# A hybrid encoder layer with 16 experts on one core: the last expert's rows stay on chip and reach the output by one-hot products

## The reference

```python
def grouped_moe(x, w_router, router_bias, wg, wu, wd):
    ...
    combine = jnp.einsum('tk,tke->te', w, jax.nn.one_hot(idx, N_EXPERTS, dtype=jnp.float32)).astype(x.dtype)
    y = jnp.zeros_like(xt)
    for e in range(N_EXPERTS):
        h = jax.nn.silu(xt @ wg[e]) * (xt @ wu[e])
        y = y + combine[:, e:e + 1] * (h @ wd[e])
    return y.reshape(shp)
...
        return layer_norm(ALPHA * x + y, ln2_g[l], ln2_b[l])
```

## Time and profile before

| what | us |
|---|---|
| median of 3 runs | 1161.46 |
| lowest, highest | 1157.88, 1167.65 |
| the profiled execution, its own time | 1164.74 |
| its span, first to last instruction | 1163.1 |
| PE, DVE, ACT, POOL busy in it | 1043.3, 894.6, 718.1, 188.7 |

### The profile page before, as it was taken

The page is one execution under the profiler, slowest core; times in us unless marked ns, Lnnn a source line. Parts: engine busy times, 40 slices in busy tenths (PEclk is TensorE's granted clock), DMA queues, the critical chain, the costliest instruction groups (busy, mean ns, idle before and its releaser), DMA issues.

```text
span 1163.1 us, 16849 instructions
## 1 busy us (share of the span) xinstructions
PE 1043.3 (90%) x5403; PEld 875.7 (75%) x5403; DVE 894.6 (77%) x1148; ACT 718.1 (62%) x887; POOL 188.7 (16%) x162
## 2 busy tenths in 40 slices
PE   5999999969989999999389999998799999999950
PEld 4988888857878888887278878887677888888840
DVE  2696674579978999887757858646897888888956
ACT  2424765356868888877524266734576888787852
POOL 3000000016421101110020000000372311221100
PEclk9999889979989999999799999899899999999985
DMA  9423120339999999997734222020799999999934
GB/s 316 160 80 110 40 78 19 110 103 318 366 344 379 387 385 384 385 375 303 222 103 145 81 83 92 27 101 27 248 303 381 376 381 392 379 379 378 374 120 163
DMA packets 117061, 273.27 MB, mean 235 GB/s; under 512 B 10304, under 2 KB 13344, under 8 KB 116992
## 3 DMA queue, kind: packets, MB, share of 16 engines
q1 hardware_dynamic: 101232, 236.80, 56.6%
q0 software_dynamic: 14464, 33.01, 8.1%
q10 hardware_dynamic: 1296, 2.62, 0.6%
HBM read 262.02 MB, written 25.22 MB: 247 GB/s over the span
## 4 chain that ended last, share of the span: by engine, by line
PE 57%; DMA 17%; DVE 10%; issue 6%; ACT 4%; DVEq 3%; POOL 3%; SPq 0%; ACTq 0%; POOLq 0%
DMA raw_far<-in_w_gate 9%; PE bankA L2093 9%; PE bankA L1801 8%; PE bankB L2093 7%; PE bankB L1801 7%; PE bankC L2116 5%; PE bankD L2116 5%; PE bankC L1801 3%; POOL slot_rows L727 3%; PE bankD L1801 3%; PE bankG L1881 3%; DVE w_lo L453 2%; PE bankE L1789 2%; PE bankF L1789 2%; ACT w_hi L447 2%
## 5 line engine op out<-in xcount | busy, mean ns | idle before, releaser
L453 DVE TENSOR_TENSOR w_lo<-raw,w_hi 128x2048 fp32r<-128x2048 f32 (+1 forms) x152 | 340.7, 2261 | 57.1 <-ACT w_hi L447 54.1
L447 ACT ACTIVATE w_hi<-raw 128x2048 fp32r<-128x2048 f32 (+1 forms) x152 | 287.1, 1893 | 120.9 <-PE bankC L1801 40.9
L453 DVE TENSOR_TENSOR w_lo<-raw_far,w_hi 128x2048 fp32r<-128x2048 f32 x64 | 146.4, 2288 | 14.5 <-ACT w_hi L447 14.5
L447 ACT ACTIVATE w_hi<-raw_far 128x2048 fp32r<-128x2048 f32 x64 | 122.8, 1919 | 46.8 <-PE bankB L2093 22.6
L2093 PE MATMUL bankA<-w_hi,xe_hi 128*128 128x512 f32 x256 | 100.7, 394 | 3.4 <-DVE xe_lo L468 3.2
L2093 PE MATMUL bankB<-w_hi,xe_hi 128*128 128x512 f32 x256 | 102.8, 402 | 0.6 <-DVE w_lo L453 0.6
L2093 PE MATMUL bankB<-w_hi,xe_lo 128*128 128x512 f32 x256 | 100.1, 391 | 0.0
L2093 PE MATMUL bankA<-w_hi,xe_lo 128*128 128x512 f32 x256 | 99.9, 390 | 0.0
L2093 PE MATMUL bankB<-w_lo,xe_hi 128*128 128x512 f32 x256 | 99.8, 390 | 0.0
L2093 PE MATMUL bankA<-w_lo,xe_hi 128*128 128x512 f32 x256 | 99.8, 390 | 0.0
L707 POOL DMA_INDIRECT y_rows<-expert_out,idx x32 | 47.9, 1495 | 189.0 <-ACT expert_out L1005 181.3
(11 more groups left out here) (430 smaller groups left out, 2459.5 us busy)
## 6 DMA issues: line engine op xcount, KB each, us to landing
raw<-in_w_up SPq DMA_DIRECT2D x64, 1024.0 KB, 11.3
raw_far<-in_w_gate SPq DMA_DIRECT2D x60, 1024.0 KB, 12.3
raw<-in_w_down SPq DMA_DIRECT2D x60, 1024.0 KB, 12.3
raw<-in_w_in SPq DMA_DIRECT2D x12, 1024.0 KB, 8.8
raw<-in_w_o SPq DMA_DIRECT2D x8, 1024.0 KB, 5.5
x_rows<-x POOLq DMA_DIRECT2D x10, 512.0 KB, 3.0
raw<-in_w_gate SPq DMA_DIRECT2D x4, 1024.0 KB, 8.2
raw_far<-in_w_down SPq DMA_DIRECT2D x4, 1024.0 KB, 12.3
```

The costliest lines, as they stand in the source:

```text
L447: act.activation(w_hi[:, s % RB, :, 0:n], raw_unit(s)[:, :, 0:n], ACT.Copy).then_inc(hi_done, 1)
L453: dve.tensor_tensor(w_lo[:, s % RB, :, 0:n], raw_unit(s)[:, :, 0:n], w_hi[:, s % RB, :, 0:n].bitcast(F32), ALU.subtract).then_inc(lo_done, 1)
```

## The change

Expert 15's output is never scattered. It is always a row's second expert, so:

- ACT and DVE split banks C and D of expert 15 into `xe_hi` and `xe_lo` (`last_hi`, `last_lo`), which stay on chip.
- POOL, in its program behind expert 11, makes five one-hot matrices `place_of[t]` [128 slots, 128 rows] from the slot list (`places`), from a copy of an iota that it loads.
- PE multiplies `place_of[t]` by `xe_hi` and `xe_lo` into two banks per tile (`last_rows`: G and H for even tiles, C and D for odd), and adds `y_second[t]` to them by a product with the identity (`second_rows`) for tiles 0 to 2 in layer 0 and for all in layer 1; DVE adds `y_second` itself for tiles 3 and 4 of layer 0. DVE adds the banks to `x` (`add_last`).
- Rows that have no scattered second output must read zero, so POOL writes zeros to all second rows of `y_rows` in each layer, by nine DMAs of 64 rows of 4 KB, right behind the store of `gv`.
- SP issues the loads of both outputs of a tile together, once expert 14's scatter has landed; the last waits for the turned hidden rows of 15.
- Down of expert 14 comes ahead of up of 15, on PE and in the order of the units. ACT and DVE follow.
- Of the next layer's first four units, two are split before `last_hi` and `last_lo` and two later; before, all came ahead of the sums but for the last `w_lo`. The first additions move into DVE's loop, two tiles ahead. PE runs 10 spare products behind down of 15. On ACT `root(0)` moves behind two copies.

The core of the diff:

```diff
+            def gate_or_up(l, s, w, e, i=0):
+                for k in range(2):
+                    load_expert(l, s + k, w[l, e, k * HALF:(k + 1) * HALF, :].rearrange("(t p) n -> p t n", t=4), i)
+
...
-                gate_up(l, SO_LAST, NE - 1)
-                down(l, SO_LAST + 4, NE - 2)
+                gate_or_up(l, SO_LAST, w_gate, NE - 1)
+                down(l, SO_LAST + 2, NE - 2)
+                gate_or_up(l, SO_LAST + 4, w_up, NE - 1)
                 down(l, SO_LAST + 6, NE - 1)
 
                 def block_units(e, b, ran):
...
-                    load_outputs(j)
+                sp.wait_ge(out_free[1], (NE // 2) * (l + 1))
+                sp.sem_inc(held_sp, 1)
+                sp.wait_ge(out_free[0], (NE // 2) * (l + 1) + 1)
+                sp.sem_inc(held_sp, 1)
+                for t in range(NT):
+                    load_output(t, 0)
+                    if t == NT - 1:
+                        wait_filled(sp, "ht", l, 0, NE - 1)
+                        sp.sem_inc(held_sp, 1)
+                    load_output(t, 1)
 
             for t in range(NT):
...
+                hold(zero_out, 16)
+                for a in range(0, SEQ + DEC, DEC):
+                    pool.dma_start(y2_dram[2 * a:2 * a + 2 * DEC, :].rearrange("(p j) n -> p j n", j=2)[:, 1, :],
+                                   zero_dram[0].partition_broadcast(DEC)).then_inc(second_zero, 16)
...
                 for e in range(NE):
                     if e + 4 < NE:
                         gather_next(e + 4)
-                    send(e)
+                    if e < NE - 1:
+                        send(e)
+                    else:
+                        pool.sem_inc(out_free[1], 1)
+                    if e == NE - 5:
+                        places()
 
                 def block_rows(e, b, ran):
 
...
                         round_end(i, c, s)
-                round_of(0, NE - 1, SO_LAST)
-                expert_rows_out(0, NE - 2)
-                hidden_hi(0, NE - 1)
+                last = NE - 1
+                split_hi(act, l, SO_LAST + 4, after="half")
+                hidden_hi(0, last - 1)
+                split_hi(act, l, SO_LAST + 5, after="gate", c=last)
+                gate(0, last)
+                split_hi(act, l, SO_LAST + 6, after="half")
+                expert_rows_out(0, last - 1)
+                split_hi(act, l, SO_LAST + 7, after="down1", c=last - 1)
+                hidden_hi(0, last)
                 def block_act(e, b, ran):
                     def hi(dst, src, after):
...
 
+                def last_hi():
+                    for h in range(2):
+                        hi_out(act, f"down{h}", l, t_cols(xe_hi, h, 1), hi_y, 0, NE - 1)
+
...
-                    expert_rows_out(0, NE - 1)
-                    with act.If(l < DEPTH - 1):
-                        for s in range(2, RB):
-                            next_split(s)
-                    act.sem_inc(held_act, 1)
-
-                overflow(act, l, past, block_act, held_act, after_blocks, lambda: expert_rows_out(0, NE - 1), no_blocks)
...
                         split_lo(dve, l, s + 9, i)
-                round_of(0, NE - 1, SO_LAST)
+                split_lo(dve, l, SO_LAST + 4)
+                hidden_lo(0, NE - 2)
+                split_lo(dve, l, SO_LAST + 5)
+                split_lo(dve, l, SO_LAST + 6)
+                split_lo(dve, l, SO_LAST + 7)
+                hidden_out(0, NE - 1)
                 hidden_lo(0, NE - 1)
 
...
+
+                def next_splits(units):
+                    with dve.If(l < DEPTH - 1):
+                        for s in units:
+                            split_lo(dve, l + 1, s)
+
+                def after_blocks(ran):
...
+                    last_lo()
+
+                overflow(dve, l, past, block_dve, held_dve, after_blocks, last_lo, no_blocks)
 
 
...
                     dve.sem_inc(held_dve, 1)
+                    add_output(t, 1, y_second[:, t, :])
+
+                def add_last(t):
                     n = P if t < 4 else DEC
-                    add_output(t, 1, y_second[:, t, :], accum_out=mv[0:n, t, 0:1])
-                    dve.drain()
-                    dve.tensor_scalar(mv[:, t, 0:1], mv[:, t, 0:1], -1.0 / D, None, ALU.mult).then_inc(mean_done, 1)
+                    dve.drain()
+                    for h in range(2):
+                        name = ("last", t, h)
+                        wait_filled(dve, name, l)
+                        part = x[0:n, t, h * HALF:(h + 1) * HALF]
+                        read(dve.scalar_tensor_tensor(out=part, in0=bank_of(name)[0:n, :], scalar=w12[0:n, t, 1:2], in1=part,
+                                                      op0=ALU.mult, op1=ALU.add, accum_out=sq[0:n, t, h:h + 1]), name)
+                    dve.drain()
+                    dve.tensor_scalar(mv[:, t, 0:1], sq[:, t, 0:1], sq[:, t, 1:2], -1.0 / D, ALU.add, ALU.mult).then_inc(mean_done, 1)
 
...
-                    for s in range(RB - 1):
-                        split_lo(dve, l + 1, s)
-
                 def tail(more):
                     dve.wait_ge(table2_in, 32 * l + 32)
                     dve.sem_inc(held_dve, 1)
-                    dve.drain()
-                    for t in range(NT):
+                    dve.memset(sq[DEC:P, NT - 1, :], 0.0)
+                    dve.drain()
+
+                    def add_before(t):
                         add_first(t)
-                    dve.memset(mv[DEC:P, NT - 1, 0:1], 0.0)
-                    dve.drain()
...
 
-                    add_second(0)
+                    add_before(0)
+                    add_before(1)
+                    add_last(0)
                     for t in range(NT):
+                        if t + 2 < NT:
+                            add_before(t + 2)
                         if t + 1 < NT:
-                            add_second(t + 1)
-
+                            add_last(t + 1)
                         dve.wait_ge(square_done, NT * l + t + 1)
                         dve.sem_inc(held_dve, 1)
                         centre_2(t)
...
                     if 2 <= t + 1 < NT:
                         turn_rows(l, t + 1)
-                    if t == 0 and between:
+                    if t == 0 and between is not None:
                         warm_products(5)
                     wait_read(pe, ("xt", t, 1), l)
                     projection(l, 0, t)
+                    if between is not None and t + SECOND_ON_PE < NT:
+                        between(t + SECOND_ON_PE, True)
                     if t == 0:
                         turn_rows(l, 1)
...
                         down(s + 4, i, c - 1)
-                round_of(0, NE - 1, SO_LAST)
-                down(SO_LAST + 4, 0, NE - 2)
+                wide("gate", SO_LAST, 0, NE - 1)
+                hidden_turn(0, NE - 2)
+                down(SO_LAST + 2, 0, NE - 2)
+                wide("up", SO_LAST + 4, 0, NE - 1)
                 hidden_turn(0, NE - 1)
...
+                overflow(pe, l, past, block_pe, held_pe, blocks_read)
+
+                def last_rows(t, stop=False):
+
+                    n = P if t < 4 else DEC
+                    for h in range(2):
+                        name = ("last", t, h)
+                        wait_free(pe, name, l)
+                        pe.sem_inc(held_pe, 1)
+                        wait_read(pe, f"down{h}", l, 0, NE - 1)
+                        for k, y in enumerate((xe_hi, xe_lo)):
+                            ins = pe.matmul(bank_of(name)[0:n, :], place_of[t][:, 0:n], t_cols(y, h, 1),
+                                            start=(k == 0), stop=(stop and k == 1))
+                        if stop:
+                            done(ins, name)
+
+                def second_rows(t):
+
+                    n = P if t < 4 else DEC
+                    pe.wait_ge(y_second_in[t], 16 * l + 16)
+                    pe.sem_inc(held_pe, 1)
+                    for h in range(2):
+                        name = ("last", t, h)
+                        done(pe.matmul(bank_of(name)[0:n, :], ident[0:n, 0:n], y_second[0:n, t, h * HALF:(h + 1) * HALF],
+                                       start=False, stop=True), name)
+
+                wait_free(pe, ("last", 0, 0), l)
+                for _ in range(10):
+                    pe.matmul(bank_of(("last", 0, 0))[:, :], h_hi[:, 0, 0:P], h_hi[:, 0:2, :], start=True, stop=True)
+                pe.wait_ge(places_done, l + 1)
+                pe.sem_inc(held_pe, 1)
+                last_rows(0)
+                last_rows(1)
+                second_rows(0)
+                second_rows(1)
 
                 with pe.If(l < DEPTH - 1):
+                    for t in range(2, SECOND_ON_PE):
+                        last_rows(t)
+                        second_rows(t)
                     wait_unit(pe, l + 1, 0)
                     wait_free(pe, ("proj", 0, 0), l + 1)
                     pe.sem_inc(held_pe, 1)
-                    pe.wait_ge(y_second_in[0], 16 * l + 16)
```

(8 more changed lines are left out.)

86 lines of the change are left out of this document (62 added, 24 removed).

## The result

The changed kernel takes 1203.72 us (median of 4 runs, 1201.61 to 1204.19), the kernel before 1163.51 beside it (4 runs). The ratio is 1.035, its 95% interval 1.0319 to 1.0382. Forecast were 1175 us and a range from 1156 to 1185: the sign is right, the size is a third of what came, and the time lies 19 us above the range. The profiled run of the change has a span of 1202.6 us, 39.5 more than that of before.

What follows compares the result with a forecast made beforehand. PE was taken as the bound, with 27 us of scatter and `y_second` waits at the layer ends, DVE next. Terms 8.5 - 0.5 + 5.4 = +13.4 us gave 1178.1 profiled, 1175 us forecast, range 1156 to 1185.

Steps and rivals of the forecast that it cites:

- the zeros, +5.4: At the first scores: zero writes delay the mask by 3.8 us in layer 1, 1.6 in layer 0; bounds 0 and 11.
- Rival (c): At the first scores: zeros cost the upper bound of 11 us in place of 5.4, giving 1180.5 us; chance 0.15.
- The loop of waits, +8.5: Layer 0's tail and next head: DVE and PE wait for each other around the projections, 8.5 us more; bounds +5 and +13.
- The order, +3.3 a layer: Last experts: down of 14 ahead of up of 15 makes down of 15 end 3.3 us later in each layer.
- The early means: Layer ends: without the scatter, tile 0's mean comes 5.6 us earlier in layer 0 and 5.0 in layer 1.
- layer 1's tail: After down of 15: additions in DVE's loop give most back; layer 1 in all -0.5 us, bounds -4 and +3.
- `root(0)`: "nothing": On ACT: moving `root(0)` behind two copies costs nothing.
- `places`, the wait for the zeros: On POOL: `places` ahead of the scatter of 12, and the wait for long-landed zeros, cost nothing; 3 us without that cover.

Runs made afterwards that it cites:

- Experiment 11: Changed kernel with zeros later, placing products before projection 0, old expert order, last layer's branch first, 22 spare products, `root(0)` back: 1156.06 us, ratio 0.9971.
- experiment 2: Kernel before, plus only the nine DMAs of zeros per layer at the change's place, read by nothing: 1177.28 us, ratio 1.0118.
- experiment 1: Changed kernel with the nine DMAs of zeros moved behind the load of `ln1_shift`, some 10 us later: 1187.08 us, ratio 1.0186.
- experiment 12: Kernel before, plus only down of 14 ahead of up of 15 on PE, ACT, DVE and in the unit order: 1161.31 us, ratio 0.9977.
- experiment 6: Changed kernel with PE's branch of the last layer written ahead of the branch with the next head: 1202.61 us, ratio 1.0323.

## Why the prediction was wrong

Of the change's 40 us, by what undoing each part gave: zeros 16.6, order 9.7, loop of waits 9.7, `root(0)` 4.9; sum 40.9. Experiment 11 took them all out, and ratio 1.035 became 0.997. Each of the four is uncertain by some 6 us, and by ratios they are 19, 12, 10 and 5, so that the sum comes within 1 us of 40 is luck.

In the profiled runs the sum had +13.4 us and +39.5 came, 26.1 more. By the table they are: 9.4 up to gate of 15 of layer 0 (11.0 for the 1.6 of the zeros), 4.7 from there to the turning of tile 4 (13.2 for 8.5), 2.3 from there to the second group of projections, where PE's idle time grew by 3.3, 4.2 at layer 1's scores (8.0 for 3.8), 3.5 from them to gate of 15, and 2.0 from there to the end (1.5 for -0.5).

**The step that failed most: the zeros, +5.4.** The mechanism was right (the mask lands late, and the first scores wait 12 us in layer 1), the term was mis-sized. Between the ends 0 and 6.7 us for the delay I took 3.8, for a third taker in turns; the mask landed 6.8 us later (15.3 for 8.5), which is the upper end. The zeros start 3 us ahead of the mask and POOL goes on issuing them for 1.3 us behind it; the delay is what it would be if nearly all of them were served first. And of layer 0's share I counted 2.2 us as hidden by the wait of the next scores; in experiment 2 the first scores come 7.0 us later and the next ones 6.9. The wait of the next scores, 1.85 us in the earlier trace rows, is still 1.74 there: PE makes them only when the first ones have been read, so that wait moves along and covers nothing. The term should have been 14 (6.8 in each layer); experiments 2 and 1 give 14.4 and 16.6. Rival (c) had this mechanism, with 11 as its upper bound, which the hidden share kept too low.

**The loop of waits, +8.5, was right in kind and short.** Both gaps came as forecast (6.65 and 6.38 us for 6.3 each), and projection 0 started 0.9 us earlier behind gate of 15 for 1.4 forecast. What came on top is the clock: I gave 1.2 us for a slower projection 2; the 4.8 us idle ahead of projection 0 cost 2.9 there, and the turns of tiles 3 and 4 and the projections in between another 2. From gate of 15 the turn of tile 4 comes 13.2 us later. That wait could have been read from the sum's own terms, in which 6.8 us lie between tile 0's being ready and its low rows; but I put a slow clock only where the kernel before had one.

**The order, +3.3 a layer.** Layer 0: 3.2. Layer 1: 4.8, the difference being down of 14 at the granted clock of 0.80. With the new order gate to down of 15 takes 22.4 or 24.0 us, whichever the layer: 24.0 in three of seven traces in layer 0 and in six of seven in layer 1. The sum had 0.3 for slow products. What I hadn't asked is what the order is good for: experiment 12 shows that beside the scatter of 15 it gives back up to 5.5 us at the first mean for the 3.2, and the change takes that scatter away. Both halves of the change attack one wait; with the first, the second has nothing left but its price.

**The early means were right**: counted from gate of 15, 5.8 us in layer 0 for 5.6 and 4.0 in layer 1 for 5.0; counted from down of 15, 9.0 and 8.9 us. In layer 1's tail I forecast that the additions in the loop would give most of it back: from down of 15 to the end 36.4 us are left of 39.8, 3.3 less, for a forecast of 3.8 less (0.5 and the 3.3 of the order).

**`root(0)`: "nothing" was wrong**, by 4.9 us in the total and 3.9 by the traces. I named no work that hides it, because it looked like two copies changing places. The price isn't in ACT's time, it is in PE's clock three steps on.

**`places`, the wait for the zeros**: next to nothing, as forecast. The rounds of the experts in which `places` runs take 18.1 us in both layers; the same rounds took 18.1 and 18.3 before.

Open: the idle time at the second group of projections (4.91 us for 1.59) is 2.9 to 5.4 us in all variants with PE's new program and 1.0 to 2.1 in those of the kernel before; experiment 6 didn't settle it.

## What to carry to other kernels

Bulk writes that nobody waits for yet still stand ahead of a small load that somebody waits for: price them at the whole time of their bytes unless something shows otherwise, and put them behind it. When an engine waits longer in a place, count the products that follow at the lower clock, also where two small operations on another engine only changed places. Before two measures are joined, ask whether they buy the same wait; the order of the last experts could pay only while expert 15 was scattered. And when a wait is removed, count the work that had run in it: here the first additions moved into the loop behind, and the loop grew by more than half of what the earlier start gave (5.5 us for 8.3 in layer 1).

## What the runs showed of the hardware

- The 24 products of tile 1 with `w_o` took 8.8 to 13.3 us in the eight traces with the moved root, behind a wait of some 2.5 us, and 7.2 to 7.6 us in the six without it, where PE didn't wait ahead of them; one of those twelve, experiment 2 in layer 0, took 8.9. I hadn't expected that 2.5 us of waiting could cost up to 6 us of slower products.
- The clock can fall without any difference in the program. In the traces of the kernel before and of experiment 12, which differ only in the last experts, PE is busy for 8.69 us of the 10 from 120 to 130 in both. From 130 on the granted clock is 0.50 in the one and 1.00 in the other, and the first product with `w_o` comes 4.4 us apart (139.51 and 135.12). Over the 14 traces that stretch, from layer 0's first scores, takes 31.5 to 37.6 us; a difference of a few us between two traces shows nothing by itself.
- The Trainium skill (DMA: Bandwidth & Descriptors, Queues, rings and completion order) has the DMA engines take turns between queue rows. The trace doesn't contradict it, but the mask, 384 KB, landed in 15.3 us with nine DMAs of 256 KB issued from 3 us ahead of it on, in 10.5 with four, and in 8.5 with none: in these runs turns didn't shield the small load. The prediction had from the same page that a delay near 6.7 us means turns made dear by large packets; 6.8 fits that, but no run here separates it from a plain queue.
